# A two-layer encoder step in fp32 on one core: 1/rms of a stage's input moved behind its projections

## The reference, cut to what matters

```python
def pre_mod(h, g_pre, shift, scale):
    return rmsnorm(h, g_pre) * (1 + scale[:, None, :]) + shift[:, None, :]

def post_add(h, y, g_post, gate, weight):
    return h + weight * gate[:, None, :] * rmsnorm(y, g_post)

def swiglu(x, w1, w2):
    g, u = jnp.split(x @ w1, 2, axis=-1)
    return (jax.nn.silu(g) * u) @ w2
```

## Time and profile before

| | |
|---|---|
| median of 3 runs | 3158.42 us (3157.22 to 6316.38) |
| profiled execution | 3162.64 us, its span 3160.9 us |
| granted TensorE clock, mean | 0.970 of 2.4 GHz |
| busy: PE / DVE / ACT / POOL | 94% / 42% / 31% / 17% of the span |
| HBM read / written | 312 MB / 11.5 MB, 102 GB/s over the span |

### The profile page before, as it was taken

How to read it: one execution, slowest core, us unless ns; L and a number is a source line. 1 busy time by engine, 2 the same in 40 slices (tenths; PEclk the granted TensorE clock), 3 DMA queues, 4 the chain that set the end, 5 groups by cost and what they waited for, 6 DMA issues and landing times.

```text
span 3160.9 us, 51132 instructions
## 1 busy us (share of the span) xinstructions
PE 2982.7 (94%) x21970; PEld 2787.3 (88%) x21970; DVE 1333.7 (42%) x1982; ACT 979.6 (31%) x1736; POOL 541.5 (17%) x558
## 2 busy tenths in 40 slices
PE   6999997999899979999989999979998999799996
PEld 5999997877799979999979999977777999799996
DVE  4222337455333672234472223475543336733321
ACT  3222223444422332223232222234443224322221
POOL 0000324000000550004240004240000005400003
PEclk9999998999999989999989999989997999899998
DMA  5444432322122224432224453222321222122221
GB/s 215 148 153 153 139 107 76 112 103 72 55 87 81 80 75 146 154 120 81 78 89 154 144 168 127 87 78 104 118 74 38 87 81 74 59 82 87 86 82 57
DMA packets 90977, 325.21 MB, mean 103 GB/s; under 512 B 11120, under 2 KB 14224, under 8 KB 90560
## 3 DMA queue, kind: packets, MB, share of 16 engines
q1 hardware_dynamic: 63936, 223.35, 21.4%
q0 software_dynamic: 26816, 98.59, 9.1%
HBM read 312.19 MB, written 11.55 MB: 102 GB/s over the span
## 4 chain that ended last, share of the span: by engine, by line
PE 65%; issue 23%; DVE 5%; POOLq 3%; POOL 2%; DMA 1%; ACT 1%; DVEq 0%; SPq 0%; ACTq 0%
PE ps L514 51%; PE ps L833 3%; PE ps L542 3%; PE ps L863 3%; PE ps L629 2%; DVE x_lo L1403 1%; PE ps L846 1%; POOLq L1797 1%; POOL h L1798 1%; DVE norm_t L1394 1%; DMA ada_first<-in_ada 1%; POOLq L1775 1%; ACT prob_t L1181 1%; POOLq L1773 1%; POOL acc_x L1791 0%
## 5 line engine op out<-in xcount | busy, mean ns | idle before, releaser
L514 PE MATMUL ps<-x_hi,w_hi 128*128 128x288 f32 x3968 | 878.0, 303 | 6.4 <-DVE next L1732 4.8
L514 PE MATMUL ps<-x_hi,w_lo 128*128 128x288 f32 x3968 | 848.2, 295 | 0.0
L514 PE MATMUL ps<-x_lo,w_hi 128*128 128x288 f32 x3968 | 847.3, 295 | 0.0
L1279 DVE TENSOR_TENSOR w_lo<-w_raw,w_hi 128x1024 fp32r<-128x1024 f32 x390 | 541.1, 1394 | 710.9 <-ACT w_hi L952 710.3
L514 PEld LDWEIGHTS ps<-x_hi,w_hi 128*128 128x128 f32 x3968 | 632.5, 189 | 77.9 <-issue 70.8
L514 PEld LDWEIGHTS ps<-x_lo,w_hi 128*128 128x128 f32 x3968 | 639.1, 189 | 0.0
L514 PEld LDWEIGHTS ps<-x_hi,w_lo 128*128 128x128 f32 x3968 | 638.8, 189 | 0.0
L952 ACT CAST w_hi<-w_raw 128x1024 fp32r<-128x1024 f32 x390 | 403.8, 1043 | 83.9 <-DMA w_raw<-in_f 69.9
L514 PE MATMUL ps<-hid_hi,w_hi 128*128 128x288 f32 x1232 | 264.3, 295 | 0.0
L514 PE MATMUL ps<-hid_hi,w_lo 128*128 128x288 f32 x1232 | 262.3, 294 | 0.0
L514 PE MATMUL ps<-hid_lo,w_hi 128*128 128x288 f32 x1232 | 262.2, 294 | 0.0
(11 more groups left out here) (221 smaller groups left out, 3631.8 us busy)
## 6 DMA issues: line engine op xcount, KB each, us to landing
w_raw<-in_f SPq DMA_DIRECT2D x264, 512.0 KB, 3.6
ada_w<-in_ada POOLq DMA_DIRECT2D x128, 512.0 KB, 5.6
w_raw<-in_gate SPq DMA_DIRECT2D x64, 512.0 KB, 3.6
w_raw<-in_tri SPq DMA_DIRECT2D x42, 512.0 KB, 3.7
decay_s<-f_scratch POOLq DMA_DIRECT2D x8, 1088.0 KB, 7.8
ada_first<-in_ada SPq DMA_DIRECT2D x4, 2048.0 KB, 21.7
w_raw<-in_wout SPq DMA_DIRECT2D x16, 512.0 KB, 3.6
decay_p<-f_scratch POOLq DMA_DIRECT2D x8, 512.0 KB, 5.6
```

Of the source, the lines that this page charges most:

```text
L514: r = mm(out[:, b, :], w, xx[:, b * HALF:(b + 1) * HALF], start=first and n == 0, stop=last and n == 2)
L1279: V.tensor_tensor(w_lo[:, s, :], w_in[:, s, :], w_hi[:, s, :], ALU.subtract).then_inc(lo_ready.sem, 1)
```

## The change

- x_hi and x_lo hold h x pre_scale, without 1/rms of h and without the shift. ACT makes x_hi straight from h, DVE x_lo. 1/rms (`r2`) is multiplied in where an accumulator leaves PSUM (`take`, on DVE; the first group's are copied out raw by ACT and scaled later).
- The shifts of prompt and sample stand as two more columns behind half 0 of x; every matmul that reads half 0 of x has 290 columns for 288, and the projected shift comes out in two columns of PSUM, is copied to `c_col` and added by the next operation. A row of x_hi and x_lo is 580 elements for 576, and half 1 begins at element 290.
- Gone: `new_square`, the second newton of each half, norm_t, the sums of z squared and z h, `square_of_h`. The squares of the new h are made by ACT, added by one reduction on DVE, summed over partitions by PE behind the first group, and r2 follows from Ln, Exp and one newton of 576 columns.
- The new h is made on DVE, in groups of one or two tiles. POOL only issues DMAs. `sum_of_y` of half 1 stands behind tile 1 of half 0 in `first_group`.
- Fillers run 11 tiles ahead at the first attention stage instead of 3; the stages end at the tiles in `STAGE_ENDS`, counted over all triples and the 16 tiles of u. The last stage has 15 filler tiles. In `before_pairs` 16 tiles of T = 1 stand ahead of the wait for nxt_full, where 4 did.
- q, k, v and the gates are taken by DVE; bias, shift and Sigmoid or Silu follow on ACT in place. Some constants move, and the gate bias is loaded per layer.

```diff
--- before.py
+++ after.py
...
+SH = 2
+XHALF = HALF + SH
+XW = 2 * XHALF
...
+def moving(b):
+    return slice(0, XHALF) if b == 0 else xcols(1)
...
-LEAD = 3
+LEAD = 11
+STAGE_ENDS = (34, 57, 79, 100, 121, (NP - 1) * TRI + 2 * KD)
...
+def stage_work(st):
+    n = STAGE_ENDS[st] - (STAGE_ENDS[st - 1] if st else LEAD)
+    out = list(WORK)
+    for at in (24, 23, 20, 18, 16, 14, 24, 12, 10):
+        if sum(out) > n:
+            out[at] -= 1
+    assert sum(out) == n and min(out) >= 0, (st, n, out)
...
-    z = sb("z", [P, KD, TOK], at=x_at)
...
+    x_lo = sb("x_lo", [P, KD, XW], F32R)
+    z = sb("z", [P, KD, XW], at=x_at)
...
+        def split_tile(out, c, t, hi, lo, cols, first, last, halves=BOTH):
...
+                for b in halves:
+                    width = cols(b).stop - cols(b).start
+                    r = mm(ps[:, 2 * out + b, 0:width], w, xx[:, cols(b)],
...
-            if boundary:
-                sum_of_y(*j, 1)
             for k in range(KD):
                 pe.wait_ge(x_ready.sem, x_ready.done(l, x_index(n, 0, k)))
                 for s in lock:
-                    split_half(pair[s], chunk(l, ph, s), k, k, x_hi, x_lo, 0, k == 0, k == KD - 1)
-                if k == 1 and boundary:
-                    sums_of_z(*j, 1)
+                    x_half(l, ph, s, k, 0)
+                if k == 1 and j[0] >= 0:
+                    sum_of_y(*j, 1)
...
+            if l or n:
+                pe.wait_ge(alt_taken.sem, alt_taken.done(l, ab == "b"))
+                sum_of_h(*((l, n - 1) if n else (l - 1, 2)), 2)
...
+        def project_ahead(l, j):
+            if j < (NP - 1) * TRI:
+                project_tile(l, 2 + j // TRI, j % TRI)
+            else:
+                project_u(l, j - (NP - 1) * TRI)
...
             first_group(l, "tri", 1, (0, 1, 2), ())
-            project(l, 1, 0, 4)
+            sum_of_h(l, 0, 3)
+            project(l, 1, 0, 2 * KD)
             pe.wait_ge(nxt_full.sem, nxt_full.done(l, 2))
...
-            project(l, 1, 4, 12)
+            project(l, 1, 2 * KD, TRI)
...
-            project(l, 1, 12, 18)
+            project(l, 2, 0, 6)
...
-            project(l, 1, 18, TRI)
-            project(l, 2, 0, LEAD)
+            project(l, 2, 6, LEAD)
...
+            if l or ab == "b":
+                first_raw(l, ab)
+                estimate_h(*((l, 1) if ab == "b" else (l - 1, 2)), 2)
...
+                    act.wait_ge(acc_free[0].sem, acc_free[0].done(l, GROUP_AT[ph][0] + i - 1))
+                for g, part in ((0, slice(0, SEQ)), (1, slice(SEQ, TOK))):
+                    r = A(sil[:, i, part], sil[:, i, part], ACT.Silu, bias=c_col[:, 2 * (i % 2), g:g + 1])
+                r.then_inc(sil_ready.sem, 1)
...
+        def first_raw(l, ab):
+            ph = "f1" + ab
+            for s, dst in enumerate((sil[:, 0, :], hid[:, 0, :], sil[:, 1, :], hid[:, 1, :])):
+                chunk_over(l, ph, s)
+                copy(c_col[:, s, :], shifted(s))
+                r = copy(two(dst), pair[s])
+                if s < 2:
+                    r.then_inc(acc_free[s].sem, 1)
+                else:
+                    r.then_inc(alt_taken.sem if s == 2 else raw_taken.sem, 1)
+                if s in (1, 2):
+                    split_hi()
+        def estimate_h(l, j, p):
+            act.wait_ge(sum_h_ready.sem, sum_h_ready.done(l, j))
+            A(two(rms[:, EST, :]), pair[p], ACT.Ln, scale=1.0 / D_MODEL, bias=eps_t[:, 0:1])
+            act.drain()
+            A(rms[:, EST, :], rms[:, EST, :], ACT.Exp, scale=-0.5).then_inc(est_h_ready.sem, 1)
...
         def make_x(l, n, b, k):
-            i, p = x_index(n, b, k), k % 3
-            act.wait_ge(t_ready.sem, t_ready.done(l, i))
             for _, g, part in spans((b,)):
-                r = A(x_hi[:, k, part], nt[:, p, part], ACT.Identity, bias=shift(l, n, k, g))
+                r = A(x_hi[:, k, xpart(b, part)], h[:, k, part], ACT.Copy, scale=pre_scale[:, n, k, g:g + 1])
             r.then_inc(x_high.sem, 1)
+        def square_h(l, j, b, k):
+            r = A(sq_h[:, k, columns(b)], h[:, k, columns(b)], ACT.Square)
+            if b == 1 and k == KD - 1:
+                r.then_inc(sq_h_ready.sem, 1)
...
+                    estimate(l, j, 0)
+                for k in range(KD):
+                    act.wait_ge(h_ready.sem, h_ready.done(l, h_index(j, b, k)))
+                    make_x(nl, n, b, k)
+                    if b == 0:
+                        if k in (1, 5, 7):
+                            split_hi()
+                        if k == 2:
+                            for p in pieces(j, 1):
+                                done(1, PIECES[j][p][0])
+                                evict(l, j, p)
+                        if k == 3:
+                            estimate(l, j, 1)
+                    if k > 3:
+                        square_h(l, j, b, k - 4)
+                for k in range(4, KD):
+                    square_h(l, j, b, k)
...
+            if l or ab == "b":
+                split_lo()
+                split_lo()
...
+                    V.tensor_tensor(sil[:, i, :], sil[:, i, :], r2[:, :], ALU.mult).then_inc(g_scaled.sem, 1)
...
+                    dve.wait_ge(chunk_done.sem, chunk_done.done(0, chunk(l, ph, 2 * i)))
+                    take(sil[:, i, :], 0, 2 * (i % 2)).then_inc(acc_free[0].sem, 1)
                     split_lo()
...
+                    take(hid[:, i, :], 1, 2 * (i % 2) + 1).then_inc(acc_free[1].sem, 1)
...
+        def take(dst, p, c):
+            V.tensor_tensor(two(dst), pair[p], two(r2[:, :]), ALU.mult)
+            return V.tensor_copy(c_col[:, c, :], shifted(p))
...
+        def add_squares_of_h(l, j):
+            dve.wait_ge(sq_h_ready.sem, sq_h_ready.done(l, j))
+            V.reduce_sum(sum_h[:, :], sq_h[:, :, :].rearrange("p k t -> p t k"), AXX).then_inc(h_summed.sem, 1)
+        def norm_of_h(l, j, p):
+            dve.wait_ge(est_h_ready.sem, est_h_ready.done(l, j))
+            newton(two(r2[:, :]), two(rms[:, EST, :]), two(rms[:, VAR, :]), pair[p])
+        def new_h(l, j, b, i):
+            k0, k1 = H_GROUPS[i]
+            r1 = rms[:, R1:R1 + 1, columns(b)].to_broadcast((P, k1 - k0, HALF))
+            V.tensor_tensor(z[:, k0:k1, xcols(b)], z[:, k0:k1, xcols(b)], r1, ALU.mult)
+            dve.drain()
+            V.tensor_tensor(h[:, k0:k1, columns(b)], h[:, k0:k1, columns(b)], z[:, k0:k1, xcols(b)], ALU.add
+                            ).then_inc(h_ready.sem, 1)
...
+                r = V.scalar_tensor_tensor(out=x_lo[:, k, xpart(b, part)], in0=h[:, k, part],
+                                           scalar=pre_scale[:, n, k, g:g + 1], in1=x_hi[:, k, xpart(b, part)],
+                                           op0=ALU.mult, op1=ALU.subtract)
...
+            new_h(l, j, 0, 0)
+            new_h(l, j, 0, 1)
+            x_low(nl, n, 0, 0)
+            new_h(l, j, 0, 2)
+            x_low(nl, n, 0, 1)
             split_lo()
-            pre_rms(l, j, 0)
-            for k in range(KD):
-                normed(nl, n, 0, k, h_tile(0))
-                if k == 0:
-                    for p in pieces(j, 1):
-                        add_y(l, j, p)
-                        add_z(l, j, p)
-                else:
-                    x_low(nl, n, 0, k - 1)
-                if k == 3:
-                    post_rms(l, j, 1)
-                    new_square(l, j, 1)
-                if k == 5:
-                    split_lo()
-                if k == 7:
-                    pre_rms(l, j, 1)
-            x_low(nl, n, 0, KD - 1)
+            x_low(nl, n, 0, 2)
+            for p in pieces(j, 1):
+                add_y(l, j, p)
+            x_low(nl, n, 0, 3)
+            new_h(l, j, 0, 3)
+            x_low(nl, n, 0, 4)
+            x_low(nl, n, 0, 5)
+            new_h(l, j, 0, 4)
+            norm_of_y(l, j, 1)
+            x_low(nl, n, 0, 6)
+            x_low(nl, n, 0, 7)
             split_lo()
-            for k in range(KD):
-                normed(nl, n, 1, k, h_tile(1))
-                if k:
-                    x_low(nl, n, 1, k - 1)
-            x_low(nl, n, 1, KD - 1)
+            dve.wait_ge(acc_free[1].sem, last_acc)
+            new_h(l, j, 1, 0)
...
+            norm_of_h(l, 0, 3)
+            for s in (2, 0, 1):
+                dve.wait_ge(*((raw_taken.sem, raw_taken.done(l, 1)) if s == 2 else
+                              (acc_free[s].sem, acc_free[s].done(l, GROUP_AT["tri"][s]))))
+                V.tensor_tensor(nxt[:, s, :], nxt[:, s, :], r2[:, :], ALU.mult)
+            dve.drain()
+            for s in (2, 0, 1):
+                for g, part in ((0, slice(0, SEQ)), (1, slice(SEQ, TOK))):
+                    V.tensor_scalar(nxt[:, s, part], nxt[:, s, part], c_col[:, s, g:g + 1], None, ALU.add)
+            dve.drain()
+            dve.sem_inc(nxt_full.sem, 3)
+            dve.wait_ge(vc_turned.sem, vc_turned.done(l, 0))
+            take_q(l, 1)
+            take_k(l, 1)
             forget(l)
...
+        def take_q(l, T):
```

(14 more changed lines are left out.)

685 lines of the change are left out of this document (293 added, 392 removed).

## The result

The changed kernel takes 3171.5 us (median of 20 runs), the kernel before 3157.4 us (20 runs on the same chips): a ratio of 1.0047, with an interval of 1.0034 to 1.0061. It is slower by 0.5%, within the 2% that count as no change here, 82.5 us from the forecast and outside its range. The profiled execution took 3171.95 us, span 3170.2, against 3162.6 and 3160.9 before: 9.3 us more.

The account below looks back on a forecast made before the run. PE was taken as the bound, busy 2982.7 of 3160.9 us, with 115 to 125 us lost at five stage boundaries. Terms summed to -69: 3162.6 becomes 3094, the median 3158.4 becomes 3089 us; range 3055 to 3128.

Parts of the forecast that it names:

- items 1 to 4: Stage boundaries before an FFN, before the mixer, out of `out`, and kernel end: -16.4, -28.6, -42.0, -9.8 us; start -1.
- item 1: Boundary before an FFN, out of an FFN, once: less DVE work and silent POOL let x start earlier, -16.4 us.
- R: Moment at a boundary when DVE has 1/rms of y for half 0; the schedule's times count from it.
- Item 5: Matmuls reading x: two more columns on half of 12,960 cost 0.9 ns each, +6 us.
- slower than before: Rival: x rows at multiples of 2320 and 1160 bytes slow all 12,960 streamed matmuls; 3232 us at 11 ns, chance 0.05.
- Item 8: Attention: q, k, v leave through DVE behind logits, so PE waits; +8 us for two layers, +20 if logits always late.
- Item 7: before_pairs: take_q and take_k now lie before forget, so PE waits for take_q and sums of f; +4 us for two.
- Item 9: Clock: falls in both layers' last attention stage, +5 us; one possible fall at the `out` boundary, +3 us.
- DVE stays slow or late: Rival: strided reduction at twice the time costs 21 us, or item 8's hand-overs cost 20; 3110 us, chance 0.20.
- The clock stays up: Rival: clock holds in both last attention stages and boundaries lose their low stretches; 3062 us, chance 0.17.
- The splits bind: Rival: chunk splits bind the first group as before, so only some half is gained; 3125 us, chance 0.12.
- the slow reads: Same rival as "slower than before": reads from the new x row starts slow the matmuls; 3232 us, chance 0.05.

Follow-up runs that it names:

- the first experiment: Kernel before with x starting 8, 16 or 32 bytes past 64 (first two also moved hid or weights), or 290 columns: 3172.5, 3156.2, 3167.9, 3173.0 us.

## Why the prediction was wrong

**The boundaries (items 1 to 4): right in mechanism, 21 us too large.** Forecast -98, measured -76. In the boundary of item 1 PE ended the first group 34.5 us after y, where the schedule said 33.0 (R+38.2 less R+5.2); DVE's operations of 288 columns took 0.51 us and those of 576 0.76, as taken. What was short: the reduction took 8.4 us, not 5.2, because its rate was taken from a row without a stride (that rate gives 5.4, not 5.2, for 4608 elements). PE stood 3.4 us before the mixer (2.3 forecast) and 2.0 at each head where chunk 3 was to cover it; the run with contiguous adds gave 10.9 us back. And at `out` PE waited 4.3 us for z, an eviction that ScalarE had queued behind three x tiles. The schedule followed DVE and did not follow ScalarE's order there.

**Item 5 is the step that failed first: +6 forecast, +32 measured.** The two columns cost some 4.5 us in the changed kernel, as said. The rest is not the columns but where rows start, and that stood among the rivals, "slower than before", with a chance of 0.05, priced at 5.3 ns to cancel the gain. That a start can do this is shown: 3.5 ns for x 8 bytes past, 1 ns for hid 32 bytes past, and 15.6 us back when the changed kernel's rows were moved. In the changed kernel the spacing rose by 2.5 ns, half the price named, and by 1.6, 3.2 and 4.5 ns in the first three FFNs, the merges and the last FFN. The rival had no row to price such a read from, and item 5 and the range then carried none of it. The last two are as large because the kernel before ran at 131.5 and 130.2 ns there. Hid, m and o were left out altogether: no step asked what lies behind x in the memory and moves when x grows.

**Item 8 failed next: +8 forecast for the attention, +37 measured, +34 of it in stage 0 (24 to 34 over five profiles).** The hand-over of q was priced by PE's own order of fillers (1.5 + 1.9 us). What take_q itself stands behind on DVE, logits(0) and (1), and that these wait for a transfer issued only after the mixing products, was not looked up, nor that five tiles instead of nine lie between these products and the stage. The trace of before had both transfers.

**Tiles ahead: not in the sum.** Some 13 us of projection moved ahead of the stages. The forecast took for granted that they come off the stages; stages 1 to 3 took 46.3 us before and 46.4 to 47.1 after.

**Item 7: +4 forecast, +12 measured.** The waits themselves are as named (later_f twice 2.3 us, take_q 1.1). Behind them the clock fell at 562.5 for 6.8 us; the rest was not followed.

**Item 9: the sign was wrong.** The last stage of layer 1 took 35.7 us at a clock of 0.95, where it had taken 51.6 between the same marks. In the four kernels of the first experiment, which leave its schedule as it was, it took 37.8 to 38.0 us: the long fall in the profile of before was one execution's, not the kernel's. A sum against one profile took it for a property.

**The rivals.** "DVE stays slow or late" had its mechanism (the strided reduction), 11 us of its 21. "The clock stays up" came in the last stage of layer 1 alone (0.95); in layer 0 its stretch up to the merge had 0.80. "The splits bind" did not come: the split of the third chunk was in time (pause 1.35 us, 0.7 forecast). Only the slow reads, at 3232, stood above 3171; the others and the forecast lay below, since each loss stood alone, and the result is three of them at once. Two sums of the prediction are off without bearing on the forecast: by its own rows the five boundaries lose 129 us, not 115 to 125, and two thirds of 0.46 with 0.17 is 0.48 for faster, not 0.56.

## What to carry over

When a tensor's rows or the tensors ahead of it change size, write down the start addresses of everything that is streamed and of the weights, and price them: 2.5 ns on 12,960 matmuls outweigh a boundary. Look at a spacing stage by stage, since a mean can hide a stage that is fast. When an engine's hand-over moves behind another step, ask what that step waits for, down to the transfer. A stretch at a low clock in one profile should be looked for in a second execution before it enters a sum.

## What the runs showed that was not expected

- The spacing of matmuls of 288 columns depends on where the operands start. For hid it is 132.3 ns with hid and the weights at multiples of 64 bytes, and 133.2 with either of them 32 past. For x in the FFNs and merges it is 133.2 ns at 32 past and 135.7 at 8 past throughout, and 133.0, 131.5 and 130.2 ns by stage at multiples of 64. The Trainium skill's gap of N/2.4 GHz + 2.5 ns (TensorE: Matmul & The Clock Gate, "Back-to-back issue gap"), which that section gives for a matmul taken by itself and not for a stream with weight loads, would be 122.5 ns for all of them; no run here shows it.
- 290 columns for 288 cost 0.3 ns in three FFNs and 1.8 to 3.1 ns where the kernel before was fast.
- POOL's multiplication of 128x288 took 862 ns for 966 beside DVE, and 694 for 791 alone, with its tensors 8 bytes past a multiple of 64.
- With a wait of 6.4 us at its start, stage 0 of layer 0 took 23.6 us more in the profiled execution; the granted clock was 1.2 GHz for 41 of the 51 us behind the wait.
